# An expert stage whose gate/up halves share three homes in turn

## The chip, the cores and the metric

The kernel runs on one core of a Trainium2 chip. A core has a matrix engine (PE, with its weight loads PEld), a vector engine (DVE), a scalar engine (ACT), a general engine (POOL), a sequencer that issues transfers (SP), and 16 DMA engines that all transfers share. The metric is the device time of one execution in microseconds (us), the median of several.

## What is computed

Two transformer blocks in a row on 256 tokens of width 1024, in float32. The change lies in the mixture of experts that ends the first block: 32 experts, of which each token uses two, each with a gate and an up matrix of 1024x256 and a down matrix of 256x1024.

```python
    combine = (g_onehot[..., None] * within[..., None, :] * g_w[..., None, None])
    combine = combine.reshape(bsz, seq, N_EXPERTS).astype(xn.dtype)

    def per_sequence(args):
        xs, cw = args
        hg = jnp.einsum('sd,edf->sef', xs, w_gate)
        hu = jnp.einsum('sd,edf->sef', xs, w_up)
        act = jax.nn.silu(hg) * hu * cw[..., None]
        return jnp.einsum('sef,efd->sd', act, w_down)
```

The expert weights are 32 x 3 MB, about 100 MB, and are read once.

## The kernel before

Each engine runs its own hand-written list of instructions, held together by semaphores. Tokens are gathered by expert. An expert has 32 places, and four experts make an item of 128 rows. The list `ITEMS` has eight main items, M0 to M7 below, and between them four overflow items, O0 to O3, whose four blocks of 32 rows go to whichever experts have more than 32 tokens. The order is M0 M1 M2 O0 M3 O1 M4 O2 M5 O3 M6 M7.

PE does for an item: gather of the token rows (L2539, for two items at once), `gate_up` in two halves over the 1024 inputs (L2563, 32 matmuls in the trace for each half), two pairs of transposes in `turn` (L2571, L2573), `down` in two parts (L2589), and `scatter` of the result into four PSUM banks (L2601). ACT and DVE do the activation between `gate_up` and `turn`, and copy the result of `down` out. The order of PE's list is written in the loop over `ITEMS`: the first half of an overflow item stands ahead of the `down` of the item before it, and its second half behind that `down`.

Weights of a main item come by SP's queue in `sp_moe`: six transfers of 2 MB (`main_in`, L612), gate and up of the first half (c = 0, 1), gate and up of the second half (c = 2, 3), and the two down parts (c = 4, 5), always in this order. SP waits before each for its place to be free (`moe_free`): c = 0, 1 for the first half of the last main item, c = 2, 3 for the second half of the item before, whichever kind it is, and c = 4, 5 for the two parts of the `down` of the item before. SP is in order, so what stands behind a waiting transfer waits too.

Weights of an overflow item come by POOL's queue in `over_rows_in` (L620): an indirect transfer for each of six pieces and four blocks, 24 of them, 128 rows of 4 KB each. The rows are chosen on the chip. For a block that no expert needs, the row numbers lie beyond the bound and the rows are skipped; in the profiled execution this holds for all 16 blocks, so these transfers move no weights, but they are issued, and PE waits for them all the same. The first half has a home of its own (`over_gu`, in `arena`); the second half is put in the same part of `ring` as the second half of the main items; the down rows use the place of the main ones.

`e.rk` is the step at which DVE has worked out the row numbers; SP and POOL start their part of the stage behind it. POOL first clears the overflow home (L984). One down part of M0, c = 4, is loaded early, ahead of three chunks of the modulation weights (L645).

## Time and profile before

| | us |
|---|---|
| median of 3 runs (1303.45 to 1305.3) | 1303.59 |
| the profiled execution | 1304.3 |
| its span, first to last instruction | 1302.6 |
| expert stage in it, first half of M0 to the last scatter | 392.8 to 686.8 |

In the rows below, times are us from the span's start. A row of the timeline gives start, duration, engine, line, operation, output and inputs, the count, and in brackets how long the engine was idle before it and who ended that. PE's clock has two levels, 1.2 and 2.4 GHz; the column PEclk gives the granted share of the higher.

### The profile page before, as it was taken

The numbers are of one execution on the slowest core, as the hardware profiler recorded it, in microseconds if no ns is written. First come the engines' busy times: TensorE is split into PE (matmuls) and PEld (weight loads), VectorE is DVE, ScalarE is ACT, GpSimd is POOL, SyncE is SP. The second block draws the span as 40 slices with busy tenths as digits, with TensorE's granted clock in tenths as the row PEclk, the third lists the DMA queues.
The fourth block names the chain that finished last, engine by engine and source line by source line (L and its number), as shares of the span: only waits on it lengthen the run. The fifth ranks groups of instructions, "written<-read, shape, count | busy, mean of one in ns | idle before, by whom it ended". The sixth has DMA issues, their size and how long they took to land.

```text
span 1302.6 us, 14670 instructions
## 1 busy us (share of the span) xinstructions
PE 1099.0 (84%) x5820; PEld 797.2 (61%) x5820; DVE 625.2 (48%) x777; ACT 343.6 (26%) x428; POOL 222.8 (17%) x273
## 2 busy tenths in 40 slices
PE   1799968999968787978864988679999976999996
PEld 1679835996433342432422867668888865888885
DVE  4557485566352112212106555547675548635343
ACT  0131033231111010100102301436453423644441
POOL 4402012001112065364003003101111112000000
PEclk9899877999969999988976988589999996999998
DMA  9897555204788987767898833034866635263630
GB/s 343 232 325 269 192 191 221 98 30 188 276 358 311 409 299 272 287 230 261 346 396 289 323 130 129 1 118 141 299 249 245 218 114 213 73 246 133 222 117 33
DMA packets 123493, 287.41 MB, mean 221 GB/s; under 512 B 25734, under 2 KB 51614, under 8 KB 123434
## 3 DMA queue, kind: packets, MB, share of 16 engines
q1 hardware_dynamic: 93938, 245.45, 50.8%
q10 hardware_dynamic: 11032, 27.33, 6.2%
q0 software_dynamic: 18464, 13.82, 3.7%
q8 instruction: 40, 0.66, 0.2%
q14 instruction: 19, 0.16, 0.0%
HBM read 334.23 MB, written 2.62 MB: 259 GB/s over the span
## 4 chain that ended last, share of the span: by engine, by line
PE 68%; DMA 10%; DVE 10%; issue 5%; POOL 3%; ACT 2%; ACTq 2%; DVEq 0%; SPq 0%; POOLq 0%
PE ps L570 28%; PE ps L2563 6%; PE ps L2225 4%; PE ps L2399 3%; PE ps L2539 3%; DMA ring<-in_w_in_dram 3%; DMA ring<-in_moe_w_gate_dram 3%; PE ps L2664 2%; PE ps L2227 2%; PE ps L2486 2%; DMA ring<-in_moe_w_up_dram,early 2%; DMA macc<-in_ada_w_dram 2%; PE ps L2589 2%; PE ps L2601 2%; POOL ring L620 1%
## 5 line engine op out<-in xcount | busy, mean ns | idle before, releaser
L575 DVE TENSOR_TENSOR ring_parts<-ring,arena_parts 128x2048 fp32r<-128x2048 f32 x65 | 146.6, 2286 | 49.5 <-ACT arena_parts L1082 43.2
L570 PE MATMUL ps<-arena_parts,macc_parts 128*128 128x512 f32 x512 | 165.9, 396 | 0.0
L2563 PE MATMUL ps<-ring,hT 128*32 128x512 f32 x640 | 88.6, 708 | 43.9 <-issue 21.6
L570 PE MATMUL ps<-arena_parts,gate_parts 128*128 128x512 f32 x288 | 115.5, 401 | 7.8 <-DVE hT_parts L575 7.8
L570 PE MATMUL ps<-ring_parts,gate_parts 128*128 128x512 f32 x288 | 114.2, 396 | 0.0
L570 PE MATMUL ps<-arena_parts,hT_parts 128*128 128x512 f32 x288 | 114.1, 396 | 0.0
L570 PEld LDWEIGHTS ps<-arena_parts,macc_parts 128*128 128x128 f32 x512 | 96.2, 188 | 19.5
L570 PE MATMUL ps<-ring_parts,macc_parts 128*128 128x512 f32 x256 | 99.8, 390 | 0.0
L2563 PEld LDWEIGHTS ps<-ring,hT 128*32 128x32 f32 x640 | 26.0, 127 | 103.9 <-issue 79.1
L1082 ACT CAST arena_parts<-ring 128x2048 fp32r<-128x2048 f32 x32 | 60.3, 1908 | 81.9 <-issue 46.4
L463 POOL TENSOR_TENSOR small<-small,nhalf 128x1 f32<-128x1 f32 x16 | 10.4, 650 | 400.8 <-DVE small L497 400.8
L570 PEld LDWEIGHTS ps<-arena_parts,gate_parts 128*128 128x128 f32 x288 | 55.6, 193 | 20.1 <-DVE hT_parts L575 8.6
L2225 PE MATMUL ps<-hT,ring 128*128 128x256 f32 x288 | 67.2, 397 | 0.0
L2225 PEld LDWEIGHTS ps<-hT,ring 128*128 128x128 f32 x288 | 57.7, 201 | 8.5
L570 PEld LDWEIGHTS ps<-ring_parts,gate_parts 128*128 128x128 f32 x288 | 55.7, 193 | 11.4
L570 PEld LDWEIGHTS ps<-arena_parts,hT_parts 128*128 128x128 f32 x288 | 55.4, 192 | 11.9
L1062 ACT CAST arena_parts<-ring 128x2048 fp32r<-128x2048 f32 x32 | 60.2, 1913 | 6.0 <-DMA ring<-in_mlp_w_dram 6.0
L575 DVE TENSOR_TENSOR macc_parts<-ps,macc_parts 128x512 fp32r<-128x512 f32 x32 | 22.1, 690 | 75.4 <-ACT macc_parts L1106 75.4
L1555 DVE SCALAR_TENSOR_TENSOR macc<-ring,ccol,macc 128x1024 f32<-128x1024 f32 x42 | 54.0, 1285 | 8.5 <-DMA ring<-in_ada_w_dram 7.1
L589 PE MATMUL ps<-ident,arena 128*128 128x128 f32 x96 | 18.7, 361 | 44.9 <-DVE arena L505 41.5
L1980 DVE TENSOR_TENSOR arena<-ps,gate 128x256 f32<-128x256 f32 x12 | 5.1, 425 | 103.2 <-ACT gate L1416 103.2
L570 PEld LDWEIGHTS ps<-ring_parts,macc_parts 128*128 128x128 f32 x256 | 48.2, 188 | 9.2
(529 smaller groups left out, 1850.3 us busy)
## 6 DMA issues: line engine op xcount, KB each, us to landing
ring<-in_mlp_w_dram SPq DMA_DIRECT2D x40, 1024.0 KB, 7.5
ring<-in_moe_w_gate_dram SPq DMA_DIRECT2D x16, 2048.0 KB, 8.1
ring<-in_moe_w_up_dram SPq DMA_DIRECT2D x16, 2048.0 KB, 19.1
arena<-in_moe_w_down_dram SPq DMA_DIRECT2D x16, 2048.0 KB, 11.4
ring<-in_ada_w_dram SPq DMA_DIRECT2D x29, 1024.0 KB, 10.5
ring<-in_mlp_w_dram ACTq DMA_DIRECT2D x24, 1024.0 KB, 7.0
arena<-in_ada_w_dram SPq DMA_DIRECT2D x15, 1024.0 KB, 6.8
ring<-in_w_in_dram SPq DMA_DIRECT2D x13, 1024.0 KB, 12.6
```

Source lines behind the costliest of these rows:

```text
L570: ins = nc.tensor.matmul(o, l, r, start=start and i == 0, stop=stop and i == 2, skip_group_check=True)
L575: return eng.tensor_tensor(lo, x, hi.bitcast(F32), ALU.subtract)
L1062: nc.scalar.copy(mlp_hi[s_], ring[:, s_, :]).then_inc(a_w2, 1)
L1082: nc.scalar.copy(mlp_hi[s_], ring[:, s_, :]).then_inc(a_w1, 1)
L1555: ins = nc.vector.scalar_tensor_tensor(acc, w[:, r, :], ccol[:, k:k + 1], acc, ALU.mult, ALU.add)
L2225: ins = nc.tensor.matmul(o, w[:, k, P * j:P * j + P], hT[:, k, :], start=k == 0, stop=k == KT - 1)
L2227: ins = nc.tensor.matmul(o, hT[:, k, P * j:P * j + P], w[:, k, :], start=k == 0, stop=k == KT - 1)
L2399: ins = nc.tensor.matmul(o, lhs[:, gi, hh], rhs[:, gi, hh], start=True, stop=True)
L2486: ins = nc.tensor.matmul(ps[:, 4 + j, :], hT[:, k, P * (j // 2):P * (j // 2) + P], w, start=k == 0, stop=k == KT - 1)
L2539: ins = nc.tensor.matmul(ps[:, 6 + i // 2, 256 * (i % 2):256 * (i % 2) + 256], xn[:, tt, P * k:P * k + P], picked[:, tt, :], start=tt == 0 ...
L2563: ins = nc.tensor.matmul(ps[rows, 4 + i % 2, :].rearrange("p (i n) -> p i n", i=2), hT[:, k, P * (i % 2) + CAPQ * j:P * (i % 2) + CAPQ * j ...
L2589: ins = nc.tensor.matmul(ps[rows, 6 + h, :], tb[:, P * f + CAPQ * j:P * f + CAPQ * j + CAPQ], down_w[:, f, j, 512 * h:512 * h + 512], star ...
```

## The change

There are now three homes for a half of gate and up weights, two in `ring` and the third made of the eight areas that were the overflow home. The 24 halves of the 12 items, main and overflow alike, are numbered n = 0 to 23 and use home n mod 3. A half may be loaded when half n - 3 has been computed. Into the third home a main half comes by eight transfers of 512 KB in place of two of 2 MB, since its areas are apart. SP's order for a main item is still first half, second half, down parts; the waits are one for each half.

The down rows of an overflow block come by one indirect transfer of 8 KB rows in place of two of 4 KB rows, so an overflow item has 20 in place of 24; `down_w` is laid out with the two parts of one expert side by side, and DVE works out a second list of row numbers (two more instructions ahead of `e.rk`). POOL no longer clears the home. Both down parts of M0 are loaded behind the last modulation chunk.

```diff
+HOMES = 3
+FILLS = {2 * i + half: sum(1 for n in range((2 * i + half) % HOMES, 2 * i + half, HOMES) if ITEMS[n // 2][0] == "main")
...
+        def main_half_in(sp, i, half):
+            q, n = ITEMS[i][1], 2 * i + half
+            s_ = n % HOMES
+            if n >= HOMES:
+                sp.wait_ge(t_gu, n - HOMES + 1)
+            for r in range(2):
+                w, h = moe_rows(2 * half + r)
+                src = w[QE * q:QE * q + QE].rearrange("e (p h t) n -> p e h (t n)", p=P, h=2)[:, :, h, :]
+                if s_ < 2:
+                    sp.dma_start(gu_w[:, 2 * s_ + r], src).then_inc(moe_in[2 * s_ + r], 16)
+                else:
+                    for b in range(QE):
+                        sp.dma_start(area(third_gu[b][r], D), src[:, b, :]).then_inc(ada2_in[r], 16)
+
+        def over_half_in(pool, i, half):
+            o, n = ITEMS[i][1], 2 * i + half
+            s_ = n % HOMES
+            pool.wait_ge(t_gu, n - HOMES + 1)
...
+        def over_down_in(pool, i):
+            o = ITEMS[i][1]
+            pool.wait_ge(t_dn, 2 * i)
+            rows = A["moe_w_down"][0].rearrange("e (p h) n -> (e p) (h n)", h=2)
             for b in range(QE):
...
+                pool.indirect_dma_start(out=area(58 + 8 * b, 2 * D), out_offset=None, in_=rows,
...
-                    for c in range(6):
-                        moe_free(sp, i, c)
-                        main_in(sp, q, c)
+                    for half in range(2):
+                        main_half_in(sp, i, half)
+                    for f in range(2):
+                        sp.wait_ge(t_dn, 2 * i - 1 + f)
+                        main_in(sp, q, 4 + f)
...
-            main_in(sp, 0, 4)
             for n in (19, 20, 21):
                 gv_chunk(sp, n)
...
-            main_in(sp, 0, 5)
+            for c in (4, 5):
+                main_in(sp, 0, c)
...
-            c.link(nc.gpsimd.memset(area(0, 4 * D), 0.0))
             for i, (kind, o) in enumerate(ITEMS):
                 if kind == "over":
-                    for n in range(6):
-                        moe_free(pool, i, n)
-                        over_rows_in(pool, o, n)
+                    over_half_in(pool, i, 0)
+                    over_half_in(pool, i, 1)
+                    over_down_in(pool, i)
...
+            c.link(nc.vector.tensor_scalar(owner[:, 16:32], owner[:, 0:16], 0.5, None, ALU.mult))
+            c.link(nc.vector.tensor_copy(idx_dn, owner[:, 16:32]))
             c.at("e.rk")
...
-                over_next = i < NI - 1 and ITEMS[i + 1][0] == "over"
+                ahead = i < NI - 1 and "over" in (kind, ITEMS[i + 1][0])
                 both_next = i % 2 and i < NI - 1
-                if kind == "main":
+                if i == 0 or "over" not in (kind, ITEMS[i - 1][0]):
                     gate_up(i, 0)
                     gate_up(i, 1)
...
-                if over_next:
+                if ahead:
                     gate_up(i + 1, 0)
                 down(i)
-                if over_next:
+                if ahead:
                     gate_up(i + 1, 1)
```

PE's list of the kernel before, from the gather behind O0's halves to the second half of M3. L2539 is the gather, L2571 and L2573 are `turn`, L2589 is `down` of O0, L2563 are M3's halves:

```order
447 L2571 MATMUL ps<-ident,arena 128x128 [waits v_sel,v_act]
448 L2571 MATMUL ps<-ident,arena 128x128
449 L2573 MATMUL ps<-ident,macc 128x128 x2
450 L2539 MATMUL ps<-arena 128x256 [waits v_hg,a_hg,v_sel]
451 L2539 MATMUL ps<-arena 128x256 x7
452 L2589 MATMUL ps<-arena,gate 32x512 [waits v_hg,over_in2,a_hg,v_turn]
...
456 L2563 MATMUL ps<-ring,hT 32x512 [waits v_hg,a_hg,v_turn,ring_in1,ring_in0]
457 L2563 MATMUL ps<-ring,hT 32x512 x15
458 L2563 MATMUL ps<-ring,hT 32x512 [waits a_hg,v_hg,ring_in3,ring_in2]
```

The same place in the changed kernel (L2575 is the gather, L2607 and L2609 `turn`, L2599 a half, L2625 `down`):

```order
449 L2609 MATMUL ps<-ident,macc 128x128 x2
450 L2575 MATMUL ps<-arena 128x256 [waits v_hg,a_hg,v_sel]
451 L2575 MATMUL ps<-arena 128x256 x7
452 L2599 MATMUL ps<-arena,hT 32x512 [waits v_hg,a_hg,v_turn,ada2_in1,ada2_in0]
453 L2599 MATMUL ps<-arena,hT 32x512 x15
454 L2625 MATMUL ps<-arena,gate 32x512 [waits v_hg,over_in2,a_hg,v_turn]
455 L2625 MATMUL ps<-arena,gate 32x512 x7
...
458 L2599 MATMUL ps<-ring,hT 32x512 [waits a_hg,v_hg,ring_in1,ring_in0]
459 L2599 MATMUL ps<-ring,hT 32x512 x15
```

M3's first half has moved ahead of O0's `down`, and reads the third home in `arena`; its second half stays behind that `down`.

SP's queue of the kernel before, from the end of the modulation chunks (L645) to M1's weights (L612; L707 are bias rows):

```order
70 L612 DMA arena<-in_moe_w_down_dram 128x4x1024
71 L645 DMA arena<-in_ada_w_dram 128x2x1024 [waits t_gv] x3
72 L612 DMA ring<-in_moe_w_gate_dram 128x4x1024 [waits t_out]
73 L612 DMA ring<-in_moe_w_up_dram 128x4x1024
74 L645 DMA arena<-in_ada_w_dram 128x2x1024 [waits t_gv] x2
75 L612 DMA arena<-in_moe_w_down_dram 128x4x1024
76 L707 DMA arena<-in_ada_b_dram 128x1024 [waits t_gv]
77 L707 DMA arena<-in_ada_b_dram 128x1024 x2
78 L612 DMA ring<-in_moe_w_gate_dram 128x4x1024 [waits t_gu,v_e]
79 L612 DMA ring<-in_moe_w_up_dram 128x4x1024 [waits t_gu]
```

The same place now (L678 are the chunks, L742 the bias rows, L629 the third home, L626 the homes in `ring`):

```order
70 L678 DMA arena<-in_ada_w_dram 128x2x1024 [waits t_gv] x3
71 L615 DMA ring<-in_moe_w_gate_dram 128x4x1024 [waits t_out]
72 L615 DMA ring<-in_moe_w_up_dram 128x4x1024
73 L678 DMA arena<-in_ada_w_dram 128x2x1024 [waits t_gv] x2
74 L615 DMA arena<-in_moe_w_down_dram 128x4x1024 x2
75 L742 DMA arena<-in_ada_b_dram 128x1024 [waits t_gv]
76 L742 DMA arena<-in_ada_b_dram 128x1024 x2
77 L629 DMA arena<-in_moe_w_gate_dram 128x1024 [waits v_e]
78 L629 DMA arena<-in_moe_w_gate_dram 128x1024 x3
79 L629 DMA arena<-in_moe_w_up_dram 128x1024 x4
80 L626 DMA ring<-in_moe_w_gate_dram 128x4x1024 [waits t_gu]
```

One down part of M0 has moved behind the last chunks, and M1's first half waits for `e.rk` (v_e) alone and no more for PE (t_gu).

POOL's queue of the kernel before for an overflow item, O1, and now:

```order
101 L620 DMA arena<-in_moe_w_gate_dram,early 128x1024 [waits t_gu]
102 L620 DMA arena<-in_moe_w_gate_dram,early 128x1024 x3
103 L620 DMA arena<-in_moe_w_up_dram,early 128x1024 [waits t_gu]
104 L620 DMA arena<-in_moe_w_up_dram,early 128x1024 x3
105 L620 DMA ring<-in_moe_w_gate_dram,early 128x1024 [waits t_gu]
106 L620 DMA ring<-in_moe_w_gate_dram,early 128x1024 x3
107 L620 DMA ring<-in_moe_w_up_dram,early 128x1024 [waits t_gu]
108 L620 DMA ring<-in_moe_w_up_dram,early 128x1024 x3
109 L620 DMA arena<-in_moe_w_down_dram,early 128x1024 [waits t_dn]
```

```order
97 L640 DMA ring<-in_moe_w_gate_dram,early 128x1024 [waits t_gu]
98 L640 DMA ring<-in_moe_w_gate_dram,early 128x1024 x3
99 L640 DMA ring<-in_moe_w_up_dram,early 128x1024 x4
100 L640 DMA arena<-in_moe_w_gate_dram,early 128x1024 [waits t_gu]
101 L640 DMA arena<-in_moe_w_gate_dram,early 128x1024 x3
102 L640 DMA arena<-in_moe_w_up_dram,early 128x1024 x4
103 L649 DMA arena<-in_moe_w_down_dram,early 128x2048 [waits t_dn]
104 L649 DMA arena<-in_moe_w_down_dram,early 128x2048 x3
```

The halves still take eight transfers each; the down rows take four in place of eight, each with rows twice as long.

## Rows read from the trace of the kernel before

**Rows 1.** Waits, 385 to 700 us: engine, line, waited for, total, times, longest.
```profile
PE ps L2563 <- issue: 21.6, 4, 7.9
PE ps L2563 <- DMA ring<-in_moe_w_up_dram,early: 21.3, 4, 6.2
```
**Rows 2.** Timeline of PE, one pair: M3's scatter, O1, M4's halves.
```profile
500.76 3.70 PE L2601 MATMUL ps<-macc,gate 128*128 128x512 f32 x8
...
504.84 3.64 PE L2563 MATMUL ps<-arena,hT 128*32 128x512 f32 x32
508.30 3.62 PE L2589 MATMUL ps<-arena,gate 128*32 128x512 f32 x32
518.10 5.96 PE L2563 MATMUL ps<-ring,hT 128*32 128x512 f32 x32 [6.19 <-DMA ring<-in_moe_w_up_dram,early]
523.99 3.70 PE L2601 MATMUL ps<-macc,gate 128*128 128x512 f32 x8
527.53 3.62 PE L2539 MATMUL ps<-arena 128*128 128x256 f32 x16
...
532.33 3.69 PE L2539 MATMUL ps<-arena 128*128 128x256 f32 x16 [0.74 <-DVE hT L1958]
537.31 3.64 PE L2589 MATMUL ps<-arena,gate 128*32 128x512 f32 x32 [1.29 <-DVE hT L1958]
540.74 7.08 PE L2563 MATMUL ps<-ring,hT 128*32 128x512 f32 x64
547.75 3.70 PE L2601 MATMUL ps<-macc,gate 128*128 128x512 f32 x8
```
**Rows 3.** Timeline of PE: second halves of M2 and O0, then M6's scatter, M7's second half.
```profile
452.01 6.57 PE L2563 MATMUL ps<-ring,hT 128*32 128x512 f32 x32 [5.58 <-issue]
...
473.43 3.64 PE L2563 MATMUL ps<-ring,hT 128*32 128x512 f32 x32 [3.77 <-DMA ring<-in_moe_w_up_dram,early]
...
640.60 3.70 PE L2601 MATMUL ps<-macc,gate 128*128 128x512 f32 x8
...
667.27 6.46 PE L2563 MATMUL ps<-ring,hT 128*32 128x512 f32 x32 [3.78 <-issue]
```
**Rows 4.** Windows of 10 us: engines, then PEclk, DMA share, GB/s.
```profile
430.00:440.00 10.00, 7.97 (x43) 6.33 (x45) 2.59 (x5) 2.04 (x4) 0.00 (x0) 1.00 1.03 410
560.00:570.00 10.00, 5.38 (x28) 1.57 (x32) 1.84 (x4) 0.00 (x0) 7.56 (x9) 0.69 0.29 80
```
**Rows 5.** Timeline of PE at the start: M1's two halves.
```profile
413.13 3.64 PE L2563 MATMUL ps<-ring,hT 128*32 128x512 f32 x32 [0.99 <-DVE early L1563]
421.18 4.93 PE L2563 MATMUL ps<-ring,hT 128*32 128x512 f32 x32 [4.41 <-issue]
```
**Rows 6.** DMA, 384 to 388 us: the end of what is queued before the stage.
```profile
DMA packets 317, 1.12 MB, mean 281 GB/s; under 512 B 43, under 2 KB 43, under 8 KB 317
```
**Rows 7.** Timeline of SP's issues of down parts, of M1 and of M6.
```profile
410.48 2.08 SPq L612 DMA_DIRECT2D arena<-in_moe_w_down_dram  x2
...
632.13 2.08 SPq L612 DMA_DIRECT2D arena<-in_moe_w_down_dram  x2
```
**Rows 8.** Timeline of POOL: first of the eight transfers of O1's second half.
```profile
501.65 0.99 POOL L620 DMA_INDIRECT ring<-in_moe_w_gate_dram,early  x1 [11.20 <-PE ps L2563]
```
**Rows 9.** DMA queues, 474 to 476 us, two indirect transfers: packets, MB, share.
```profile
q0 software_dynamic: 288, 0.00, 6.3%
```
**Rows 10.** DMA queues, 506 to 508 us.
```profile
q1 hardware_dynamic: 186, 0.76, 95.4%
q0 software_dynamic: 163, 0.00, 4.8%
```
**Rows 11.** DMA queues, 510 to 512 us.
```profile
q1 hardware_dynamic: 194, 0.78, 99.1%
q0 software_dynamic: 194, 0.00, 5.9%
```
**Rows 12.** DMA, 731 to 738 us, where transfers of 512 KB are queued.
```profile
DMA packets 778, 2.87 MB, mean 410 GB/s; under 512 B 78, under 2 KB 78, under 8 KB 778
```

More of the change, by code:

```diff
@@ L47 @@
 N_PIECES = 48
-LAST_BEFORE = {kind: [max([j for j in range(i) if ITEMS[j][0] == kind], default=-1) for i in range(NI)]
-               for kind in ("main", "over")}
+HOMES = 3
+FILLS = {2 * i + half: sum(1 for n in range((2 * i + half) % HOMES, 2 * i + half, HOMES) if ITEMS[n // 2][0] == "main")
+         for i in range(NI) for half in range(2)}
+HOME2_FILLS = sum(1 for n in range(2, 2 * NI, HOMES) if ITEMS[n // 2][0] == "main")
 FIN = {key: i + 1 for i, key in enumerate([(0, 0), (2, 0), (0, 1), (0, 2), (2, 1), (2, 2), (1, 1), (1, 2), (1, 0),
@@ L256, in program @@
         idx = pick_i[:, :].rearrange("p (h b) -> p h b", h=2)
+        idx_dn = early[:, 640:656].bitcast(I32)
         sel_w = [macc[:, 2, 256 * i:256 * i + 256].rearrange("p (a s) -> p a s", a=TT) for i in range(4)]
@@ new lines, in over_half_in @@
+        def over_half_in(pool, i, half):
+            o, n = ITEMS[i][1], 2 * i + half
+            s_ = n % HOMES
+            pool.wait_ge(t_gu, n - HOMES + 1)
+            for r in range(2):
+                w, h = moe_rows(2 * half + r)
+                rows = w.rearrange("e (p h t) n -> (e p h) (t n)", p=P, h=2)
+                for b in range(QE):
+                    home = gu_w[:, 2 * s_ + r, b, :] if s_ < 2 else area(third_gu[b][r], D)
+                    pool.indirect_dma_start(out=home, out_offset=None, in_=rows,
+                                            in_offset=bass.IndirectOffsetOnAxis(ap=idx[:, h, QE * o + b:QE * o + b + 1], axis=0),
+                                            bounds_check=NE * 2 * P - 1, oob_is_err=False).then_inc(over_in[half], 16)
@@ new lines, in half_landed @@
+        def half_landed(pe, i, half):
+            kind, o = ITEMS[i]
+            n = 2 * i + half
+            if kind == "over":
+                pe.wait_ge(over_in[half], 32 * QE * (o + 1))
+            elif n % HOMES < 2:
+                for r in range(2):
+                    c = 2 * (n % HOMES) + r
+                    pe.wait_ge(moe_in[c], len(range(c, len(stream), RING)) * 16 + 16 * (FILLS[n] + 1))
+            else:
+                for r in range(2):
+                    pe.wait_ge(ada2_in[r], 96 + 16 * QE * (FILLS[n] + 1))
@@ L712, in program @@
         mod1_done = gv_in
-        mod1_base = [b + 96 for b in gv_base]
+        mod1_base = [b + 96 + (16 * QE * HOME2_FILLS if s_ < 2 else 0) for s_, b in enumerate(gv_base)]
         def mod1_piece(n):
@@ L2544, in gate_up @@
             def gate_up(i, half):
-                for c_ in (2 * half, 2 * half + 1):
-                    moe_landed(pe, i, c_)
+                half_landed(pe, i, half)
+                home = (2 * i + half) % HOMES
                 pe.wait_ge(a_hg, 2 * (i // 2) + half + 1)
@@ L2557, in gate_up @@
                         rows = slice(CAPQ * j, CAPQ * j + CAPQ)
-                        if half == 0 and ITEMS[i][0] == "over":
-                            kb, step = over_gu[j][0], over_gu[j][1] - over_gu[j][0]
-                            w = area(kb, 2 * step * KB).rearrange("p (i n) -> p i n", i=2)[:, :, FE * k:FE * k + FE]
+                        if home == 2:
+                            kb, step = third_gu[j][0], third_gu[j][1] - third_gu[j][0]
+                            w = area(kb, 2 * step * KB).rearrange("p (i n) -> p i n", i=2)[:, :, FE * (k % 4):FE * (k % 4) + FE]
                         else:
-                            w = gu_w[:, 2 * half:2 * half + 2, j, FE * (k % 4):FE * (k % 4) + FE]
+                            w = gu_w[:, 2 * home:2 * home + 2, j, FE * (k % 4):FE * (k % 4) + FE]
                         ins = nc.tensor.matmul(ps[rows, 4 + i % 2, :].rearrange("p (i n) -> p i n", i=2), hT[:, k, P * (i % 2) + CAPQ * j:P * (i % 2) + CAPQ * j + CAPQ], w,
```

40 lines of the change are left out of this document (13 added, 27 removed).

## The prediction

> **What bounds it now.** I read the waits of PE over the stage first. Two kinds stand out, four times each, both ahead of a half of gate and up [rows 1]: a wait for the overflow item's indirect transfers, up to 6.2 us, and one the profile calls issue, up to 7.9 us, which by its place is the wait for SP's weights at the start and the end.
>
> Then the timeline of PE over one pair of items [rows 2]. The pair takes 547.75 - 500.76 = 46.99 us. By the starts: scatter and turn 4.08, O1's first half 3.46, down with the wait behind it 9.80, O1's second half 5.89, scatter 3.54, gather and turn 4.80, second gather with 1.29 of waiting 4.98, down 3.43, M4's two halves 7.01. The second half is slow: 5.89 where a half takes 3.46. The granted clock was 0.69 in the stretch that holds the same half one pair later [rows 4], so part of it ran at 1.2 GHz in place of 2.4. It had fallen behind the idle time: after 3.77 us idle a half still took 3.64, after 4.41 it took 4.93, after 5.58 it took 6.57 [rows 3, 5]. Three pairs lie between 500.76 and 640.60 [rows 2, 3], 139.84 us.
>
> DMA carries 410 GB/s when it is full [rows 4], so 2 MB (2.097e6 bytes) take 5.1 us and a main item's 12.6 MB take 30.7. That is far under 46.99 for a pair: in the middle of the stage PE's order and its waits bound, not bandwidth. At the start and in the tail the order is turned: PE waits for transfers there [rows 3, 5].
>
> **The change, the pairs.** The second half of an overflow item is now put in the home that the first half of the main item before it has left. Call the end of that half R. Behind R stand down 3.43, the main item's second half 3.50, scatter and turn 4.08, the overflow first half 3.46, and down 3.46: PE comes for the rows at R + 17.9. Before, their place was released only at the end of the main item's second half, and PE came 11.2 us behind that (518.10 - 6.19 - 500.76 [rows 2]).
>
> When do they land? POOL starts 0.9 us after the release (500.76 to 501.65 [rows 2, 8]). An indirect transfer is 144 packets [rows 9], eight are 1152. Beside a full SP queue they are served at 97 per us [rows 11]. The 163 packets of 506 to 508 [rows 10] put the first at 506.3, 4.7 after POOL's start. So 0.9 + 4.7 + 11.9 = 17.5 to the last packet. For its completion I add an estimate, 2.2: SP's chain from 632.13 to the half at 667.27 took 35.1 for six transfers of 5.1 [rows 3, 7], which leaves 4.4 for start and finish together, and I take half. That gives R + 19.7, a wait of **1.8**. The lower end is what was measured, 500.76 to 518.10 = 17.3 [rows 2], no wait, but SP's queue ran dry within it; the upper end is the whole 4.4, R + 21.9, a wait of 4.0. I take 19.7 because M4's down parts and the next half keep the queue full through the whole of it.
>
> The half behind a wait of 1.8 stays at the full clock. So of the pair go 9.80 - 3.46 = 6.34 and 5.89 - 3.46 = 2.43. The 1.29 goes too: the down that waited for DVE's copy of the second gather now has the main item's first half ahead of it, which needs the first gather alone. 46.99 - 10.06 = 36.9, plus 1.8 is 38.7. DMA's 30.7 still fit. Three pairs: 139.8 - 116.2 = **23.6** gained.
>
> SP's down parts are issued behind the first part of the overflow down, about R + 2, and land at R + 2 + 10.2 + 4.4 = R + 16.6, for a second part at R + 16.2: 0.4 of waiting that only shortens the wait for the rows, so nothing. Down rows in four transfers have some 19 us, and the two DVE instructions lie in DVE's idle time ahead of the gather's copy; nothing for both. POOL's clearing was off the path.
>
> **The start.** Before the stage the SP queue ends at about 386.7 [rows 6]. M0's early down part moves behind the last chunks, which adds 5.1: 391.8. M1's first half, now free to start at e.rk, follows to 402.1, its second half to 412.3. PE begins M1 at 413.13 as before, for that waits for DVE [rows 5]; the second half no longer waits (the 4.41 goes, and 1.4 of slow clock). But M1's down parts are issued at 410.5 as before [rows 7] and M2's weights stand behind them: 412.3 + six transfers, 30.7, + 2.8 for the finish (an estimate again, the larger share of the 4.4, as SP's start is quick) = 445.9 for M2's second half, where it was 452.01 [rows 3]. Its first half ends at 440.3 (446.4 before, by 452.01 - 5.58, less the 6.0 that M1 gains: 4.6 of start and 1.4 of slow clock), so it waits 5.6 and is slow as before. Gain so far 6.1. At O0's second half, 473.43 before, the 3.77 and a little of issue go (its rows: 440.3 + 19.7 = 460.0, PE comes at 463.4): gain 10.0. With one 1.29: **11.3** at 500.76.
>
> **The tail.** M6's down parts wait for the down of O3, and M7's halves stand behind them in SP's queue. Before, the issue was at 632.13, 8.5 ahead of the end of M6's halves at 640.60, and M7's second half started 26.7 behind it. Now M6's second half follows the down of O3: the issue is only 3.46 + 1.73 - 0.2 = 5.0 ahead, and 35.1 later is 30.1 behind. **3.5 lost.** From there on all is as before.
>
> Sum: 11.3 + 23.6 - 3.5 = 31.4. The profiled execution took 1304.3, so 1272.9; the median of the runs is 0.7 under it: **1272**.
>
> The third home is filled by eight transfers of 512 KB. Where such transfers are queued the trace shows 410 GB/s [rows 12], the same as for 2 MB [rows 4], so I add nothing. The Trainium skill speaks against it (DMA: Bandwidth & Descriptors, Anatomy of one DMA): a fixed cost of about 2.0 us for each DMA beside its bytes. If these added up, an estimate from that page is 8 x 3.2 = 25.6 us for a fill in place of 10.2, and with two such fills on the path (M2's and M7's second halves) the sum would be 1303.
>
> **Rivals.** A, the rows land as they were measured, R + 17.3, and the pairs take 36.9: 5.4 less, 1267, down to 1260 if the start gains a little more. For it: the measured landing; against it: SP's queue ran dry while it came, and one pair later too (80 GB/s over the stretch of O2's landing [rows 4]).
>
> B, the rows come later still. If an 8 KB row is two packets where a 4 KB row was one, the four down transfers bring 512 packets more, and POOL's queue is no longer empty when the second half's transfers come: 1088 + 1152 + 1152 packets at 97 per us are 35.0 us, begun 15.1 before R (down is 20.7 before R, then 0.9 and 4.7), so R + 19.9 and 2.2: a wait of 4.2. At 4 and over the clock falls, 2.4 more. 3 x (2.4 + 2.4) = 14.4: 1286. The upper end of the completion time gives the same. The Trainium skill speaks of packets of 4096 bytes at best (DMA: Bandwidth & Descriptors, SWDGE vs HWDGE vs iDMA); but no row of 8 KB is in this trace, and these rows carry nothing.
>
> C, the small transfers don't overlap and eat the gain: each with the 4.4 of start and finish over its 1.3, 8 x 5.7 = 45.6 a fill, 35.4 over 10.2, on the path twice: 71 lost and 31 gained, 1343. The row with 410 GB/s speaks against it.
>
> D, slower, one mechanism: the completions of POOL's queue don't come while SP's is full. The landings in the trace lie in stretches where SP's queue has run dry [rows 4], and none is seen under a full one. Now it is full from R + 3.6 for 31 us and more; landing at R + 37 is a wait of 19, with the clock 20 more than I count: 3 x 20 - 31 = 29 slower, 1333. It decides from a landing at R + 28. Against it: POOL's packets were served one for one beside SP's [rows 10, 11].
>
> **Chances.** Forecast, 1266 to 1279: 0.55. A, 1260 to 1266: 0.17. B, to 1290: 0.13. C 0.03. D 0.05. Elsewhere 0.07, mostly further down. The range 1261 to 1288 leaves out about 0.18. A measurement can tell 0.2%, 2.6 us, from no change. Faster 0.91, same 0.01, slower 0.08.
>
> **What would show it.** Right: the second half of O1 to O3 starts about 2 us behind the down ahead of it and takes 3.5; the pairs take 38 to 39; M1's second half follows its first; M2's starts near 446; M7's second half starts 30 behind the end of M6's. Wrong: waits over 4 with halves of 5 to 6 us behind them (B, D), a third home whose transfers run under 400 GB/s (C), or a stretch in which PE waits for DVE's copies in the new order.

## The result, and the profile after

The changed kernel takes 1269.97 us (median of 4 runs, 1268.28 to 1271.99), the kernel before 1304.44 beside it (4 runs, 1303.45 to 1308.51). The ratio is 0.973, 95% interval 0.970 to 0.976: 34.5 us faster. 1272 was predicted, 1261 to 1288 as the range. The profiled execution took 1268.28 us, with a span of 1266.6, where it was 1304.3 and 1302.6: 36.0 us of span.

The timeline of PE over the same pair as in [rows 2], M3's scatter to M4's; L2599 is now the line of the halves, L2625 down, L2575 the gather, L2637 the scatter:

```profile
487.71 3.70 PE L2637 MATMUL ps<-macc,gate 128*128 128x512 f32 x8
...
491.78 3.64 PE L2599 MATMUL ps<-ring,hT 128*32 128x512 f32 x32
495.24 1.90 PE L2625 MATMUL ps<-arena,gate 128*32 128x512 f32 x16
497.36 1.92 PE L2625 MATMUL ps<-arena,gate 128*32 128x512 f32 x16 [0.22 <-DMA arena<-in_moe_w_down_dram]
500.06 3.64 PE L2599 MATMUL ps<-arena,hT 128*32 128x512 f32 x32 [0.77 <-DMA arena<-in_moe_w_up_dram,early]
503.63 3.70 PE L2637 MATMUL ps<-macc,gate 128*128 128x512 f32 x8
507.16 3.62 PE L2575 MATMUL ps<-arena 128*128 128x256 f32 x16
...
511.96 3.69 PE L2575 MATMUL ps<-arena 128*128 128x256 f32 x16 [0.74 <-DVE hT L1992]
515.58 3.64 PE L2599 MATMUL ps<-ring,hT 128*32 128x512 f32 x32
519.04 3.62 PE L2625 MATMUL ps<-arena,gate 128*32 128x512 f32 x32
522.48 3.62 PE L2599 MATMUL ps<-ring,hT 128*32 128x512 f32 x32
526.02 3.70 PE L2637 MATMUL ps<-macc,gate 128*128 128x512 f32 x8
```

The wait of 6.19 ahead of O1's second half is 0.77, its 5.96 us are 3.64, and the 1.29 ahead of the down is gone. The pair takes 526.02 - 487.71 = 38.31; the next two start from 526.02 and take 38.19 and 37.73, 114.23 in all for 139.84.

The same timeline at M1's two halves, M2's second half, and from M6's scatter to M7's second half, which answers to [rows 3, 5]:

```profile
412.18 3.64 PE L2599 MATMUL ps<-arena,hT 128*32 128x512 f32 x32 [0.98 <-DVE early L1597]
415.61 3.64 PE L2599 MATMUL ps<-ring,hT 128*32 128x512 f32 x32
...
445.05 5.82 PE L2599 MATMUL ps<-arena,hT 128*32 128x512 f32 x32 [5.48 <-issue]
...
601.94 3.70 PE L2637 MATMUL ps<-macc,gate 128*128 128x512 f32 x8
...
611.49 1.92 PE L2625 MATMUL ps<-arena,gate 128*32 128x512 f32 x16 [2.70 <-DMA arena<-in_moe_w_down_dram]
621.77 6.21 PE L2599 MATMUL ps<-ring,hT 128*32 128x512 f32 x32 [8.36 <-issue]
632.03 6.19 PE L2599 MATMUL ps<-arena,hT 128*32 128x512 f32 x32 [4.05 <-issue]
```

M1's second half doesn't wait any more. M2's and M7's still do, and run slowly behind it.

PE's waits for the overflow rows over the stage, with the 21.3 us of [rows 1] to compare:

```profile
PE ps L2599 <- issue: 17.9, 3, 8.4
PE ps L2599 <- DMA ring<-in_moe_w_up_dram,early: 0.9, 2, 0.6
PE ps L2599 <- DMA arena<-in_moe_w_up_dram,early: 0.8, 1, 0.8
```

Twelve more runs followed, on four chips, B to E; the place of the first pair of traces is called A. On B to E the kernel before took 1315 to 1325 us and not 1304, the changed one (run on D and E alone) 1272 to 1276. So results are compared on one chip, or by the length of the stage in the traces, from the start of M0's first half to the end of the last scatter. It is 294.0 us in the trace of before and 257.7 in that of after; the difference, 36.3, is the whole gain. One execution of e6_early_down (1286.8) and one of the kernel before on chip C (1339.0) fell into a slower state and are left out of the medians.

| kernel | chip | median us | before there | ratio, 95% | stage us |
|---|---|---|---|---|---|
| changed, first trace | A | 1269.97 | 1304.44 | 0.970 to 0.976 | 257.7 |
| e1_old_order | B | 1294.25 | 1321.93 | 0.970 to 0.984 | 280.8 |
| e2_order_alone | B | 1326.00 | 1321.93 | 1.000 to 1.007 | 319.6 |
| e3_down_two_runs | B | 1289.57 | 1321.93 | 0.969 to 0.983 | 280.7 |
| e4_all_small | B | 1277.03 | 1321.93 | 0.959 to 0.973 | 266.5 |
| e5_tail | C | 1268.67 | 1323.96 | 0.955 to 0.964 | 260.0 |
| e6_early_down | C | 1273.38 | 1323.96 | 0.961 to 0.970 | 263.3 |
| e7_start | C | 1274.39 | 1323.96 | 0.958 to 0.968 | 263.9 |
| e8_all | C | 1268.08 | 1323.96 | 0.954 to 0.961 | 259.2 |
| e9_before_here | D | 1316.91 | 1315.46 | 0.998 to 1.005 | 305.2 |
| e10_after_here | D | 1271.68 | 1315.46 | 0.961 to 0.972 | 265.3 |
| e11_after_beside | E | 1275.69 | 1325.38 | 0.957 to 0.967 | 267.3 |
| e12_tail_beside | E | 1270.29 | 1325.38 | 0.952 to 0.962 | 259.9 |

### The profile page after: what moved, and what is told of

Its sections match the earlier page's. It is cut to its first block, busy times and chain, and to the rows that moved or that the text cites. A ratio compares the mean times of both kernels' runs of the same rounds, so it can differ in the third digit from the quotient of the medians.

```text
span 1266.6 us, 14671 instructions
## 1 busy us (share of the span) xinstructions
PE 1087.7 (86%) x5820; PEld 791.3 (62%) x5820; DVE 625.4 (49%) x779; ACT 343.1 (27%) x428; POOL 203.4 (16%) x256
## 3 DMA queue, kind: packets, MB, share of 16 engines
q0 software_dynamic: 16160, 13.81, 3.8%
## 4 chain that ended last, share of the span: by engine, by line
PE 67%; DMA 11%; DVE 10%; issue 4%; POOL 3%; ACT 2%; ACTq 2%; SPq 1%; DVEq 0%; POOLq 0%
PE ps L573 29%; PE ps L2599 5%; PE ps L2261 4%; PE ps L2435 3%; PE ps L2575 3%; DMA ring<-in_w_in_dram 3%; PE ps L2700 2%; PE ps L2263 2%; PE ps L2522 2%; PE ps L2637 2%; DMA macc<-in_ada_w_dram 2%; DMA ring<-in_moe_w_up_dram,early 1%; DMA ring<-in_moe_w_gate_dram 1%; DMA arena<-in_moe_w_gate_dram 1%; PE ps L2625 1%
## 5 line engine op out<-in xcount | busy, mean ns | idle before, releaser
L573 PE MATMUL ps<-arena_parts,hT_parts 128*128 128x512 f32 x288 | 114.2, 397 | 0.0
L2599 PE MATMUL ps<-ring,hT 128*32 128x512 f32 x512 | 60.5, 616 | 9.3 <-issue 8.4
L573 PEld LDWEIGHTS ps<-ring_parts,macc_parts 128*128 128x128 f32 x256 | 48.2, 188 | 9.2
L2575 PE MATMUL ps<-arena 128*128 128x256 f32 x192 | 46.9, 401 | 7.4 <-DVE hT L1992 4.9
L2625 PE MATMUL ps<-arena,gate 128*32 128x512 f32 x384 | 44.3, 594 | 6.2 <-DMA arena<-in_moe_w_down_dram 3.2
```

The source lines that it names most:

```text
L573: ins = nc.tensor.matmul(o, l, r, start=start and i == 0, stop=stop and i == 2, skip_group_check=True)
L2575: ins = nc.tensor.matmul(ps[:, 6 + i // 2, 256 * (i % 2):256 * (i % 2) + 256], xn[:, tt, P * k:P * k + P], picked[:, tt, :], start=tt == 0 ...
L2599: ins = nc.tensor.matmul(ps[rows, 4 + i % 2, :].rearrange("p (i n) -> p i n", i=2), hT[:, k, P * (i % 2) + CAPQ * j:P * (i % 2) + CAPQ * j ...
L2625: ins = nc.tensor.matmul(ps[rows, 6 + h, :], tb[:, P * f + CAPQ * j:P * f + CAPQ * j + CAPQ], down_w[:, j, f, 512 * h:512 * h + 512], star ...
```

## The experiments

**One part undone: PE's order.** The changed kernel with PE's order of before; homes, fills and down rows as changed.

```diff
-                ahead = i < NI - 1 and "over" in (kind, ITEMS[i + 1][0])
+                ahead = i < NI - 1 and ITEMS[i + 1][0] == "over"
...
-                if i == 0 or "over" not in (kind, ITEMS[i - 1][0]):
+                if kind == "main":
```

> The changed kernel with PE's list as it was before: both halves of a main item behind the down of the overflow item. Homes, queues and transfers stay as changed. Theory (time between release and use): the place of an overflow second half is released at R, the end of the main item's first half; PE now comes for it at R + 14.5 and the rows land at R + 19.2, so each of the three pairs waits some 4.7 and its half is 1 to 2.4 us slow by the clock, and the 1.29 for the gather's copy is back: a pair of about 44.8 in place of 38.1. Three pairs + 20, the 1.29 of O0 + 1, the tail - 3.5, since M6's down parts are issued 8.5 ahead of the end of its halves again: about 1288. Rival (the homes alone carry the gain, the order only saves the 1.29 four times): 1272.

Measured 1294.25, against 1277.03 for e4_all_small on the same chip, the nearest to the changed kernel there, which itself was not run on chip B: 17 us, where 18 were expected (1288 against 1270). The timeline of PE shows the wait back, 3.92 here, then 3.55 and 3.00, with a half at the slow clock behind each:

```profile
511.46 4.18 PE L2625 MATMUL ps<-arena,gate 128*32 128x512 f32 x32
519.56 5.34 PE L2599 MATMUL ps<-arena,hT 128*32 128x512 f32 x32 [3.92 <-DMA arena<-in_moe_w_up_dram,early]
```

From this row the next second half of an overflow item is 564.23 - 519.56 = 44.7 away, as worked out (44.8). That the total fits is in part luck: the three pairs from M3's scatter to M6's are 13.1 longer than those of e4_all_small (133.4 against 120.4), not 20, since its pairs take 40.1 here and not 38.1; the stage up to M3's scatter is 4.9 longer, not 1; and behind M6's scatter it is 3.7 shorter, as said (3.5). Without the new order the work between R and the rows is too short to cover them; all the rest of the change together is worth 27.7 us against the kernel before on that chip.

**One part alone: PE's order in the kernel before.**

```diff
-                over_next = i < NI - 1 and ITEMS[i + 1][0] == "over"
+                over_next = i < NI - 1 and "over" in (kind, ITEMS[i + 1][0])
...
-                if kind == "main":
+                if i == 0 or "over" not in (kind, ITEMS[i - 1][0]):
```

> The kernel before with only PE's list changed: a main item's first half ahead of the overflow item's down. Theory (time between release and use): the overflow second half still waits for the end of the main item's second half, 11.0 ahead of its use, and its 6.2 of waiting stays; the order saves 1.29 four times and costs 3.5 in the tail: 1303, within 1300 to 1305. Rival (the order carries the gain): 1285 or less.

Measured 1326.00, 0.4% over the kernel before (interval 0.0 to 0.7%): no gain, as the theory said, and a small loss that it did not have. PE's wait for the rows stays, now 7.09 in one pair, since their place is released by the end of the main second half in both orders. In the timeline of PE behind it, the second gather waits 5.93 for DVE's copy of the first, and nothing stands ahead of it.

```profile
529.30 4.95 PE L2563 MATMUL ps<-ring,hT 128*32 128x512 f32 x32 [7.09 <-DMA ring<-in_moe_w_up_dram,early]
...
547.71 6.04 PE L2539 MATMUL ps<-arena 128*128 128x256 f32 x16 [5.93 <-DVE hT L1958]
```

That copy is itself late: it starts at 546.57, 5.2 us behind the end of the first gather (537.72 + 3.62), and in the last pair, where it is not late, the wait is 0.74. So this wait is one of the late starts described below and not a price of the order; two pairs have it, and without it the loss may not be there.

So the change without the order gives 27.7 of 44.9 us on chip B and the order alone nothing. The 27.7 are not the homes alone: they hold the single run of the down rows too, whose worth on this chip the next experiment shows, and homes without either were not run. What is left of the gain needs both, a home that is free earlier and an order that puts other work between its release and its use.

**The down rows in eight transfers again.** The changed kernel, each overflow expert's down rows as two runs of 4 KB rows.

```diff
-            rows = A["moe_w_down"][0].rearrange("e (p h) n -> (e p) (h n)", h=2)
-            for b in range(QE):
-                pool.indirect_dma_start(out=area(58 + 8 * b, 2 * D), out_offset=None, in_=rows,
-                                        in_offset=bass.IndirectOffsetOnAxis(ap=idx_dn[:, QE * o + b:QE * o + b + 1], axis=0),
+            rows = A["moe_w_down"][0].rearrange("e f n -> (e f) n")
+            for h in range(2):
+                for b in range(QE):
+                    pool.indirect_dma_start(out=area(58 + 8 * b + 4 * h, D), out_offset=None, in_=rows,
+                                            in_offset=bass.IndirectOffsetOnAxis(ap=idx[:, h, QE * o + b:QE * o + b + 1], axis=0),
```

> The changed kernel with the down rows of an overflow block fetched as before, by two indirect transfers of 4 KB rows, so eight in place of four for each overflow item. Theory (only POOL's issue time counts): POOL is busy 5.2 us longer behind the down, and reaches the second half's transfers 0.85 later than now; POOL's packets that are still unserved are worked off while SP's queue is idle. Each pair + 0.9: 1272 to 1273. Rival (the backlog of packets carries over): 3 us and more for each pair, 1280 or more. Rival (it is hidden wholly): 1270.

Measured 1289.57, 12.5 us over e4_all_small beside it. I had put this part of the change at nothing; that was wrong on this chip. But the rival's mechanism is not in the trace either: PE waits for no overflow rows at all. What it shows is a PE that runs dry. The weight loads of PE (PEld) at the end of a main first half and the start of the down, where rows of four loads stand 0.43 us apart as a rule:

```profile
525.03 0.30 PEld L2600 LDWEIGHTS ps<-ring,hT 128*32 128x32 f32 x3 [0.31 <-issue]
526.62 0.14 PEld L2600 LDWEIGHTS ps<-ring,hT 128*32 128x32 f32 x2 [1.29 <-issue]
527.88 0.11 PEld L2626 LDWEIGHTS ps<-arena,gate 128*32 128x32 f32 x1 [1.12 <-issue]
528.77 0.11 PEld L2626 LDWEIGHTS ps<-arena,gate 128*32 128x32 f32 x1 [0.78 <-issue]
529.48 0.11 PEld L2626 LDWEIGHTS ps<-arena,gate 128*32 128x32 f32 x1 [0.61 <-issue]
530.18 0.11 PEld L2626 LDWEIGHTS ps<-arena,gate 128*32 128x32 f32 x1 [0.59 <-issue]
```

and POOL's row of the last of 16 transfers without a pause, begun at 507.94:

```profile
527.76 0.99 POOL L640 DMA_INDIRECT arena<-in_moe_w_up_dram,early  x1 [0.30 <-issue]
```

In this pair PE's granted clock was 1.00 throughout, and SP's queue was empty from 524 to 532 (0 GB/s), so it was neither the clock nor bandwidth. The scatters of M3 to M6 lie 45.0, 44.5 and 41.7 apart, 131.2 in all, where e4_all_small has 120.4. That is 10.8 of the 14.2 by which its stage is longer; most of the rest, 3.5, lies ahead of M3's scatter. The changed kernel has runs of 12 transfers in this place. That a longer run of POOL's transfers is what starves PE fits, but one kernel shows only that they come together. What eight transfers cost on chip A, which showed no late starts, was not tried.

**Small transfers everywhere.** All fills of main halves by eight transfers of 512 KB, not only those of the third home.

```diff
                 if s_ < 2:
-                    sp.dma_start(gu_w[:, 2 * s_ + r], src).then_inc(moe_in[2 * s_ + r], 16)
+                    for b in range(QE):
+                        sp.dma_start(gu_w[:, 2 * s_ + r, b, :], src[:, b, :]).then_inc(moe_in[2 * s_ + r], 16)
```

> The changed kernel with every main half filled by eight transfers of 512 KB, also in the two homes in ring (M0 is left as it is). Theory (queued transfers overlap their fixed costs): no change, 1270, at most 1 more. Rival (a fixed cost for each transfer adds up): at least 15 us for each of the fills on the path, M1's second half with M2's first at the start and M7's first half in the tail: 1300 or more.

Measured 1277.03, where 1270 was reckoned from chip A, and a stage of 266.5 us where the changed kernel has 265.3 and 267.3 on chips D and E. The rival's 1300 and more is far off. The stage of the changed kernel has 48 such transfers, this one 112, and it is no longer for them, as far as stages on different chips can tell.

**The tail.** M7's first half goes ahead of M6's down parts in SP's queue, and ahead of M6's down on PE.

```diff
                     for half in range(2):
-                        main_half_in(sp, i, half)
+                        if not (i == NI - 1 and half == 0):
+                            main_half_in(sp, i, half)
+                    if i == NI - 2:
+                        main_half_in(sp, i + 1, 0)
...
-                ahead = i < NI - 1 and "over" in (kind, ITEMS[i + 1][0])
+                ahead = i < NI - 1 and ("over" in (kind, ITEMS[i + 1][0]) or i == NI - 2)
...
-                if i == 0 or "over" not in (kind, ITEMS[i - 1][0]):
+                if i == 0 or (i < NI - 1 and "over" not in (kind, ITEMS[i - 1][0])):
```

> The changed kernel with M7's first half ahead of M6's down parts in SP's queue, and computed ahead of M6's down on PE. Theory (the tail is bound by SP's queue, which idles some 7 us while M6's down parts wait for the down of O3): M7's first half fills that gap, M7's second half starts near 625.6 in place of 632.0, and the stage ends 6 us earlier: 1264. Rival (the queue was the slower for the order, not the gap; M6's down now comes late, its last part at 615.4 where it was 611.5, and holds up the rest): 1270 or more.

Measured 1268.67, where 1264 was expected from chip A's time and 1270 or more by the rival. The timeline of PE from M6's second half to the last scatter:

```profile
611.18 3.62 PE L2602 MATMUL ps<-ring,hT 128*32 128x512 f32 x32
...
618.80 3.64 PE L2602 MATMUL ps<-ring,hT 128*32 128x512 f32 x32
...
626.15 1.92 PE L2628 MATMUL ps<-arena,gate 128*32 128x512 f32 x16 [1.99 <-DMA arena<-in_moe_w_down_dram]
636.43 6.25 PE L2602 MATMUL ps<-arena,hT 128*32 128x512 f32 x32 [8.36 <-issue]
...
652.09 3.67 PE L2640 MATMUL ps<-macc,gate 128*128 128x512 f32 x8 [0.91 <-DVE macc L2030]
```

M7's first half (618.80) has no wait where it had 8.36, and the stretch takes 655.76 - 611.18 = 44.6; in the trace of after it was 598.39 to 651.30, 52.9. One slow half is left of two.

**The start.** In e6_early_down half of M0's down rows (two experts of four) are loaded early, into a place that is free by then, so that less stands ahead of M1's weights in SP's queue.

```diff
+        def first_down_in(sp, e0):
+            for h in range(2):
+                src = A["moe_w_down"][0][e0:e0 + 2].rearrange("e (p h) n -> p e h n", h=2)
+                sp.dma_start(down_w[:, e0:e0 + 2, h], src[:, :, h, :]).then_inc(m0_in, 16)
...
+            first_down_in(sp, 0)
             for n in (19, 20, 21):
...
-            for c in (4, 5):
-                main_in(sp, 0, c)
+            first_down_in(sp, 2)
```

> The changed kernel with half of M0's down rows (two of four experts, both parts, 2 MB) loaded ahead of the last modulation chunks again, where DMA is idle. Theory: the queue ahead of M1 is 5.1 shorter, but M1's down parts are issued at 409.5 all the same and M2 stands behind them, so only 1.3 is gained: 1268.7. Rival (M2's second half follows the length of the queue): 5 us of its wait and the slow clock behind it, 1263.

e7_start has in addition M2's first half ahead of M1's down parts:

```diff
                     for half in range(2):
-                        main_half_in(sp, i, half)
+                        if (i, half) != (2, 0):
+                            main_half_in(sp, i, half)
+                    if i == 1:
+                        main_half_in(sp, 2, 0)
```

> The kernel with M0's early down rows, and M2's first half ahead of M1's down parts in SP's queue. Theory: the queue is full from 387 to M2's second half, ten transfers of 2 MB, so that half starts near 442.7 in place of 445.05, and as its wait is then 3.3 it is not slow: 4.7 less than the changed kernel, 1265. Rival (M1's down comes too late instead, as its second part lands at 432.4 for a use at 434.2): no gain over the kernel with the early rows alone.

e8_all is e7_start with the tail of e5_tail.

> Both: M0's early down rows with M2's first half ahead of M1's down parts, and M7's first half ahead of M6's down parts and M6's down. Theory: the two ends of the stage are independent, 4.7 and 6.3 add up: 1259.

1273.38, 1274.39 and 1268.08: all three over what I expected, by 5, 9 and 9 us, of which the other chip may have 2 to 6 (the changed kernel takes 1271.7 and 1275.7 on D and E, 1270.0 on A). e6 and e7 are within 1 us of each other; the tail makes the difference to e8, and e8 is no better than e5_tail alone. The wait ahead of M2's second half was 5.48 in the trace of after; it is 5.54 in e6, 2.65 in e7 and 0.70 in e8:

```profile
442.43 3.64 PE L2610 MATMUL ps<-arena,hT 128*32 128x512 f32 x32 [0.70 <-issue]
```

So the load that came early did not bring M2's weights forward in e6. The reason is the one in its theory: M1's down parts were issued at 411.28 all the same, and from 410 to 412 the DMA engines were nearly idle (92 GB/s, where the trace of after has 375). Where the order brought them forward, in e8, M2's scatter came 53.6 us into the stage where e5_tail has 59.3: 5.6 gained. But the next wait takes most of it, that for O0's rows, with the slow clock behind it:

```profile
459.92 5.34 PE L2610 MATMUL ps<-ring,hT 128*32 128x512 f32 x32 [2.25 <-DMA ring<-in_moe_w_up_dram,early]
```

It ends 18.2 behind the end of M2's first half, where its place came free. By M3's scatter 1.8 are left of the 5.6, by M6's nothing (219.2 us into the stage, against 218.9). M2's second half moved forward, but the release from which O0's rows count did not: it came 49.4 us into the stage here (442.43 - 0.70 - 392.35), 48.2 in e5_tail. In e7, M3's scatter is still 3.1 us ahead of e6's (93.8 and 96.9 into the stage), but its three pairs take 121.8 and those of e6 118.2: the trace of e6 has one late start, of the kind described below, of 1.8 us where e7 has 5.1. One trace of each can't part the order's gain from such differences.

**The same kernels on another chip.** By then six traces had starts that came late and that the first two did not have, so the two kernels of the study were run unchanged.

> The kernel before, with nothing changed, run for its profile beside the others. In the traces of six of the edited kernels there are once per pair of items starts of ScalarE, SyncE's queue and VectorE that come 3 to 5 us after the end of the matmul that releases them (534.83 for an end at 529.8), which neither of the first two traces has, and the comparisons of the kernel before gave 1322 and 1324 us in place of 1304. If that belongs to where they were run and not to the edits, this one shows it too: 1322 us (1314 to 1333), pairs of about 53 us in place of 47.0, as in the kernel with the new order alone, and the new order alone is then worth nothing against it. If it belongs to the edits, this trace is the first one again: pairs of 47.0, no late start, and the new order alone costs 6 us per pair.

> The changed kernel, with nothing further changed, beside the kernel before on the same chip. If late starts belong to the place: pairs of 40.4 us as in the kernel with the small transfers and the one with the other tail (38.2 in the first trace of the changed kernel), 1275 to 1278 us, ratio to the kernel before 0.963 to 0.967. The small transfers (1277.0) then cost nothing, the other tail (1268.7) is worth 7 us and the single run of the down rows (1289.6 without it) 13. If the late starts belong to the edits: pairs of 38.2 and 1270 us, so that the small transfers cost 7 us and the tail is worth only 1.

1316.91 for the kernel before and 1271.68 for the changed one, a ratio of 0.967. The late starts are in both, and they were in neither on chip A, so where (or when) a kernel runs decides whether they come. The sizes were off: the kernel before has pairs of 48.6 us on the mean and not 53, so the order alone (51.6 in e2_order_alone, on another chip) is not shown to be free there, and the changed one has 39.9 and is 3 us under the range for it. Beside one more run of the changed kernel the tail was measured again:

> The changed kernel again with nothing further changed, as the measure for the one run beside it. 1270 to 1276 us. In its trace the stretch from the start of M6's second half to the end of the last scatter takes 52 to 53 us (52.9 in its first trace, 52.0 in its second).

> The kernel in which M7's first half is loaded ahead of M6's down rows and multiplied ahead of M6's down projection. Its first trace had 44.6 us from the start of M6's second half to the end of the last scatter, against 52.9 and 52.0 in the changed kernel. If that is a gain of its own, it is 7 to 8 us faster than the changed kernel beside it, whatever the place: 1263 to 1268 us. The rival: the first comparison (1268.7 against 1271.7 elsewhere) shows the true size, since the earlier M7 half takes 6 us of the transfers' time from M6's down rows and the rest after the stage waits for other rows; then it is 1 to 4 us faster, and the gap before the first instruction of the next stage is longer by the difference.

1275.69 and 1270.29, 5.4 us apart; the ranges, 1268.7 to 1279.2 and 1262.5 to 1271.6, overlap a little. In the traces the stretch from M6's second half to the end of the last scatter takes 52.0 and 44.9, 7.1 less. In the second trace the stage begins 2.3 later, for a reason ahead of it that the edit doesn't touch, and the spans are 4.6 apart (1274.5, 1269.9). So the tail is worth about 7 in its stretch; the median says 5.4, between the theory's 7 to 8 and the rival's 1 to 4. The rival's mechanism is not there: the gap ahead of PE's first instruction behind the stage is 11.83 in the one and 11.82 in the other. e12_tail_beside is the kernel to keep: 0.957 of the kernel before on its chip, where the changed kernel is 0.962.

A late start, in the trace of e11_after_beside: the timelines of ScalarE and of SP, an activation and an issue that both wait for M4's second half.

```profile
536.04 0.38 ACT L1450 ACTIVATE gate<-ps 128x256 f32<-128x256 f32 x1 [7.39 <-remote]
```

```profile
536.03 0.37 SPq L626 DMA_DIRECT2D ring<-in_moe_w_gate_dram  x1
```

and the timeline of PE there:

```profile
527.34 3.64 PE L2599 MATMUL ps<-ring,hT 128*32 128x512 f32 x32
530.91 3.70 PE L2637 MATMUL ps<-macc,gate 128*128 128x512 f32 x8
536.99 0.50 PE L2607 MATMUL ps<-ident,arena 128*128 128x128 f32 x2 [2.38 <-DVE arena L2016]
```

The half ends at 530.98; both start 5.05 us later, at the same moment, and for the first the profile knows no releaser ("remote"). In the first trace of after the same activation stands at

```profile
526.16 0.38 ACT L1450 ACTIVATE gate<-ps 128x256 f32<-128x256 f32 x1 [2.85 <-PE ps L2599]
```

0.06 behind the end of its half (522.48 + 3.62). With two engines released together, it is the signal for both that is late and not either engine; the ends of matmuls are modelled, but PE's own next matmuls show no gap. It costs 2.4, 2.4 and 2.6 ahead of the transpose in the three pairs, 7.4 in all; the three pairs take 611.08 - 489.12 = 122.0 here and 114.2 in the first trace.

What the moments have in common is POOL. Its last transfer ahead of these two starts is

```profile
533.56 0.99 POOL L640 DMA_INDIRECT ring<-in_moe_w_up_dram,early  x1 [0.30 <-issue]
```

which ends at 534.55, and they come 1.5 behind it. In the traces of e4 to e8 and e10 to e12 there are 47 starts of ScalarE or VectorE that are 1.8 us or more late, and 44 of them come 1.3 to 1.9 behind the end of a run of POOL's transfers, at whatever moment PE had finished. It looks as if some signals get through only when the run is over. It is not shown: most of PE's signals within such a run are on time, all of them are on chip A (the activation at 526.16 lies within a run from 520.05 to 530.10), and no kernel took the transfers away.

## Why the prediction was right

**The rows' landing, R + 19.7.** Measured from the end of the main first half, taken as the start of the down behind it, to the start of the overflow second half: 480.73 to 500.06 is 19.3, then 519.04 to 538.25 is 19.2 and 557.23 to 575.97 is 18.7. The pieces, for O2: POOL started 1.0 behind R (519.04 to 520.05). Its first packets came in the half microsecond from 525.5, its last in the quarter from 537.5:

```profile
q0 software_dynamic: 8, 0.00, 0.9%
q0 software_dynamic: 1, 0.00, 0.2%
```

They were the end of what the DMA queues did from 536 to 538 us, where SP had 200 packets beside them:

```profile
q1 hardware_dynamic: 200, 0.82, 102.8%
q0 software_dynamic: 28, 0.00, 0.8%
```

So the first packet took some 5.7 us from POOL's start, not 4.7, and the completion 0.5 to 0.8 behind the last packet, not 2.2. The two errors nearly cancel, and that the landing fits within 0.4 to 1.0 is luck in that part. The measured 17.3 of before (rival A) had an empty SP queue for part of the way, and the lean to a later landing under a full one was right.

**The wait, 1.8.** The second half started at R + 19.3, and PE came at R + 18.6, that is 17.9, the 0.22 for down rows, and some 0.4 for the end of a down that nothing overlaps (497.36 + 1.92 = 499.28): what was left was 0.77, 0.61 and 0.29. The forecast of the pair, 38.7, is 38.1 on the mean; the pairs gave 25.6, not 23.6. The wait of 0.4 for SP's down parts was 0.22, 0.26 and none, and it shortened the other as said.

**The start, 11.3.** M1's second half ran without a wait, M2's started at 445.05 (forecast 445.9) behind 5.48 of waiting (5.6) and was slow. At O1's mark the gain was 500.76 - 487.71 = 13.05. Of the difference of 1.75, 0.85 is that M2's weights were there earlier, and 0.75 that M2's second half took 5.82 and not 6.57 as before; the forecast had taken its slow clock over unchanged. M1 began 0.95 earlier too, at 412.18, as the matmuls ahead of M0's down ran at the full granted clock (1.00 from 402 to 408 us, where it was 0.73 and 0.71), but what that gave ended in the wait ahead of M2's second half.

**The tail, -3.5.** M7's second half started 632.03 - 601.94 = 30.09 behind M6's scatter, forecast 30.1, before 26.7; M6's down parts were issued 5.0 ahead of that scatter (596.92), as worked out. The sum is 13.05 + 25.6 - 3.4 = 35.2 at M7, and 36.0 in the span, for the 31.4 of the forecast. That the medians come nearer, 1270.0 for 1272, is luck: the forecast was 4.6 too high for the profiled execution (1272.9, measured 1268.3) and took the median to be 0.7 under it, where it was 1.7 over.

**Small transfers, nothing.** The third home's eight transfers for M7's second half stand behind M6's down parts and the two transfers of M7's first half. PE shows when each fill had landed: M6's second down part at 611.49, M7's first half, two transfers of 2 MB, at 621.77, its second, eight of 512 KB, at 632.03. The fills take 10.28 and 10.26 us. The window of the trace in which the small ones move (after PEclk the DMA share, then GB/s) has the full rate:

```profile
620.00:630.00 10.00, 6.21 (x32) 1.55 (x32) 0.00 (x0) 0.00 (x0) 0.00 (x0) 0.65 1.03 409
```

Against the reading of the Trainium skill by which a fixed 2.0 us would add up (DMA: Bandwidth & Descriptors, Anatomy of one DMA), the measurement decides: in a queue that is kept full the eight transfers take what two did. The page's fit is for one transfer, of the kind that POOL issues; these are SP's.

**The rivals.** B: the packets of POOL's queue went from 18464 to 16160,

```profile
q0 software_dynamic: 16160, 13.81, 3.8%
```

2304 fewer, which is the 16 transfers that are gone times 144. So a transfer of 8 KB rows is no more packets than one of 4 KB rows, for rows that are skipped; rows that carry data were not tried. B's price for the clock, which begins at a wait of 4, did not hold in later runs: in e7_start a half behind a wait of 2.65 took 5.34, and [rows 3] has one of 6.46 behind 3.78. C fell with the fills just shown and e4_all_small. D: at 528 to 530 us, within the landing of O2's rows, both queues were served one for one,

```profile
q1 hardware_dynamic: 209, 0.79, 99.7%
q0 software_dynamic: 208, 0.00, 6.1%
```

and the completion came at R + 19.2, not behind SP's queue. A did not come: the pairs are 1.2 us over its 36.9 and 0.6 under the forecast, and the rows landed at R + 19.1 on the mean, not at R + 17.3.

**What the prediction did not have.** It put the down rows in one run at nothing. On chip B that part is worth 12.5 us, for a reason that is not in the trace of before. And it named a stretch in which PE waits for DVE's copies as a way to be wrong: on chip A there is none, and on the others it is 0.2 per pair in the changed kernel, with 2.4 more for DVE's product behind a late ScalarE. The 5.93 in e2_order_alone is a late start too.

## What to carry to other kernels

Where a load waits for a place, reckon from the release of the place to the use of the data, and compare that with the work which PE has between the two. Freeing the place earlier and moving work into the gap are one change in two parts: on chip B the first, with the down rows in one run, gave six tenths of the gain, the second alone none. A wait can cost more than its length: behind waits of 0.3 to 0.8 us a half took 3.64, behind 2.65 (e7_start) and 3.92 (e1_old_order) it took 5.34, and behind 6.19 (the kernel before) 5.96, at a granted clock of 0.60 to 0.69. And a gain ahead of a wait that counts from a release is kept only as far as it moves that release.

## What the runs showed of the hardware

Engines that PE releases can start 5 us late. All twelve later traces, on four chips and of both kernels, have late starts, but not the same ones. The changed kernel and the edits that keep its order (e3 to e8, e10 to e12) have them at the same places of a pair, mostly DVE's second copy of a gather 2.9 us late and ScalarE and SP behind a main item's second half 5.1 us late; with e3's longer runs DVE's copy is 4.2 to 7.2 late. e1_old_order has one, of 2.9; the kernel before (e9) has DVE's copy 2.5 to 3.5 late in three pairs and ScalarE by less than 1 there; e2_order_alone has 5.2 and 5.0 for DVE and 3.7 and 3.5 for ScalarE. Most come 1.3 to 1.9 us behind the end of a run of POOL's indirect transfers. In the longest run, of 16 transfers with e3_down_two_runs, PE's own loads came one in 0.7 to 1.3 us. On chip A neither kernel shows any of it with the same transfers. What POOL's work, the chip and the order of PE's list each do to it was not told apart. Where late starts come, the stage is 11 us longer for the kernel before (294.0 to 305.2) and 8 to 10 for the changed one (257.7 to 265.3 and 267.3), and the ratio went from 0.973 to 0.967 and 0.962. An indirect transfer whose rows are all out of bounds still costs its 144 packets and 1.3 us of POOL, and they share the queues one for one with 4 KB packets that carry data.
